# A three-layer fp32 kernel on one core: a new order of weights, exchange and compressed keys, one weight chunk loaded earlier, and modulation sums spread between contraction steps

## What is computed

```python
# layer 1: gated linear attention, 4 heads, chunks of 64 tokens
p = rms_norm(x, pre_norm[0]) @ gla_w_in
q, k, v, glr, z = split(p)
gk = log_sigmoid(glr @ w_gk_up + b_gk) / 16
o = rms_norm(gla_chunked(q, k, v, gk), head_norm) * silu(z)
x = x + rms_norm(o @ gla_w_out, post_norm[0])
# layer 2: sparse attention, 16 heads in 4 groups
p = rms_norm(x, pre_norm[1]) @ nsa_w_in
q, kc, vc, ks, vs, kw, vw, gl, z = split(p)
q, kc, ks, kw = rope(q), rope(kc), rope(ks), rope(kw)
kcmp = silu(blocks(kc, pe_k) @ ck_w1) @ ck_w2      # compressed keys
vcmp = silu(blocks(vc, pe_v) @ cv_w1) @ cv_w2      # compressed values
out = attention over (kcmp, vcmp), (ks, vs) and (kw, vw)
o = sum over the three of sigmoid(gl + b_gate) * out, * silu(z)
x = x + rms_norm(o @ nsa_w_out, post_norm[1])
# layer 3: its input is modulated by a vector c
mod = silu(c) @ w_ada + b_ada          # 1024 -> 3072: shift, scale, gate
h = rms_norm(x, norm_gain) * (1 + scale) + shift
... stick-breaking attention, causal pooling, branches, merge ...
return rms_norm(x + gate * out, final_gain)
```

## Time and profile before

| what | value |
|---|---|
| median of 3 runs | 1273.76 us (1271.89 to 1274.53) |
| profiled execution: time, span of the core | 1273.72 us, 1272.0 us |
| mean granted TensorE clock, share of full speed | 0.99 |
| PE busy | 1229.7 us (97%) |
| PEld busy | 1018.7 us (80%) |
| DVE busy | 641.5 us (50%) |
| ACT busy | 581.6 us (46%) |
| POOL busy | 349.6 us (27%) |
| DMA traffic | 111.68 MB, mean 88 GB/s |

### The profile page before, as it was taken

How to read it: one execution, slowest core, us unless ns; L and a number is a source line. 1 busy time by engine, 2 the same in 40 slices (tenths; PEclk the granted TensorE clock), 3 DMA queues, 4 the chain that set the end, 5 groups by cost and what they waited for, 6 DMA issues and landing times.

```text
span 1272.0 us, 19160 instructions
## 1 busy us (share of the span) xinstructions
PE 1229.7 (97%) x7630; PEld 1018.7 (80%) x7630; DVE 641.5 (50%) x1206; ACT 581.6 (46%) x1127; POOL 349.6 (27%) x172
## 2 busy tenths in 40 slices
PE   7999999898989999899999999999999999999998
PEld 6799868897977755566899888888888788888897
DVE  4487645476466567898735133333333581102434
ACT  4434333524422267788744544444444312434333
POOL 2344420310023211100022422223222553434441
PEclk9999999999989999999999999999999999999999
DMA  7325404454377402100022321222222223332221
GB/s 227 120 67 187 144 1 141 158 157 146 107 135 133 100 20 48 34 2 2 1 67 67 106 83 45 66 67 66 67 68 66 66 99 99 99 116 100 85 82 66
DMA packets 131200, 111.68 MB, mean 88 GB/s; under 512 B 38802, under 2 KB 128016, under 8 KB 131120
## 3 DMA queue, kind: packets, MB, share of 16 engines
q1 hardware_dynamic: 129600, 106.84, 28.7%
q10 hardware_dynamic: 1520, 3.72, 1.3%
HBM read 104.78 MB, written 2.10 MB: 84 GB/s over the span
## 4 chain that ended last, share of the span: by engine, by line
PE 72%; issue 13%; DVE 7%; POOL 4%; ACT 3%; DMA 0%; ACTq 0%; SPq 0%; POOLq 0%; DVEq 0%
PE banks L1260 34%; PE banks L1251 8%; PE banks L1283 5%; POOL w_lo L605 4%; PE banks L1805 3%; PE banks L1657 3%; PE banks L1674 3%; PE banks L1689 3%; PE banks L1712 2%; PE banks L1350 2%; PE banks L1768 2%; DVE w_lo L1908 2%; PE banks L1819 1%; PE banks L1849 1%; PE banks L1227 1%
## 5 line engine op out<-in xcount | busy, mean ns | idle before, releaser
L605 POOL TENSOR_TENSOR w_lo<-raw,w_hi 128x1024 fp32r<-128x1024 f32 x138 | 338.8, 2476 | 831.7 <-ACT w_hi L680 819.7
L1260 PE MATMUL banks<-act_hi,w_hi 128*128 128x512 f32 x704 | 279.0, 396 | 5.2 <-DVE w_lo L1908 5.1
L1260 PE MATMUL banks<-act_hi,w_lo 128*128 128x512 f32 x704 | 276.7, 393 | 0.0
L1260 PE MATMUL banks<-act_lo,w_hi 128*128 128x512 f32 x704 | 276.5, 393 | 0.0
L680 ACT ACTIVATE w_hi<-raw 128x1024 fp32r<-128x1024 f32 (+1 forms) x164 | 162.8, 1042 | 137.0 <-PE banks L1260 87.8
L1260 PEld LDWEIGHTS banks<-act_hi,w_hi 128*128 128x128 f32 x704 | 133.7, 190 | 34.5 <-issue 6.6
L1260 PEld LDWEIGHTS banks<-act_lo,w_hi 128*128 128x128 f32 x704 | 133.6, 190 | 28.5
L1260 PEld LDWEIGHTS banks<-act_hi,w_lo 128*128 128x128 f32 x704 | 133.8, 190 | 27.3
L1251 PE MATMUL banks<-w_hi,act_hi 128*128 128x256 f32 x384 | 109.1, 284 | 0.0
L1251 PE MATMUL banks<-w_hi,act_lo 128*128 128x256 f32 x384 | 108.7, 283 | 0.0
L1251 PE MATMUL banks<-w_lo,act_hi 128*128 128x256 f32 x384 | 108.7, 283 | 0.0
(11 more groups left out here) (379 smaller groups left out, 2371.2 us busy)
## 6 DMA issues: line engine op xcount, KB each, us to landing
raw<-w_in SPq DMA_DIRECT2D x32, 1024.0 KB, 5.7
raw<-gla_w_in SPq DMA_DIRECT2D x11, 1024.0 KB, 5.3
raw<-nsa_w_in SPq DMA_DIRECT2D x33, 256.0 KB, 4.5
raw<-nsa_w_in SPq DMA_DIRECT2D x6, 1024.0 KB, 5.2
raw<-gla_w_out SPq DMA_DIRECT2D x4, 1024.0 KB, 10.9
ada_first<-w_ada SPq DMA_DIRECT2D x4, 1024.0 KB, 8.5
raw<-nsa_w_out SPq DMA_DIRECT2D x16, 256.0 KB, 4.4
raw<-w_branch_a SPq DMA_DIRECT2D x4, 1024.0 KB, 5.1
```

The lines of the kernel that those rows point to most:

```text
L605: pool.tensor_tensor(w_lo[:, u, k], raw[:, u, k], w_hi[:, u, k].bitcast(F32), ALU.subtract).then_inc(lo_done, 1)
L1260: mm = pe.matmul(b[:], w[:, u, k, m * P:(m + 1) * P], x[:, k, :], start=(k == 0 and n == 0), stop=(k == KT - 1 and n == 2))
```

## The change

Five places are edited, all before the attention loop of layer 2.

1. SP loads the third chunk of the output weights of layer 1 (15) directly behind the second, and the fourth (16) ahead of modulation pieces 6 and 7. Before, both stood behind pieces 6 and 7.
2. `modulation` is called piece by piece through a new argument `beside` of `product`, ahead of single contraction steps in the m = 1 half: pieces 0 to 5 in chunk 11, pieces 6 to 9 in chunk 19. Pieces 0 to 5 go to bank 1 in place of bank 4.
3. On ACT the split of chunk 19 stands ahead of `swap_halves(0)`, that of chunk 20 ahead of `swap_halves(2)`, and `swap_halves(4)` moves from behind the split of chunk 22 to behind that of chunk 24. On DVE `turn_parts(C_KW)` moves behind the low parts of chunks 22 and 23.
4. The compressed keys are computed between the two halves of chunk 24, not between chunks 23 and 24. On DVE the low part of chunk 25 moves ahead of the copy of the compressed keys.
5. The first q chunk (28) gets a buffer of its own, `raw_first_q`, in a part of `silu_z2`, and is loaded (four DMAs with runs of 256 bytes) between chunks 23 and 24. The sums of pieces 10 and 11 move from there to `side`.

```diff
@@ SP
                 if c0 == C_GOUT:
                     load(c0, c0 % 2, m, at)
                     load(c0 + 1, (c0 + 1) % 2, m, at + CW)
+                    load(c0 + 2, c0 % 2, m, at + 2 * CW)
                     sp.wait_ge(o_read, 2 * GH)
                     load_row(rows1[:, 0], "post0")
                     load_row(rows1[:, 1], "pre1")
+                    load(c0 + 3, (c0 + 1) % 2, m, at + 3 * CW)
                     sp.wait_ge(h_ready, 2 * KT)
                     load_ada(2)
-                    load(c0 + 2, c0 % 2, m, at + 2 * CW)
-                    load(c0 + 3, (c0 + 1) % 2, m, at + 3 * CW)
                     load_ada(1)
...
                     load(c0, c0 % 2, m, at)
                     if c0 == C_KC:
                         load_ada(1)
+                    elif c0 == C_VS:
+                        sp.wait_ge(ada_summed, ADA_EARLY)
+                        load_heads(w2, N_Q, 0, raw_first_q[:], first_q_landed)
@@ ACT
             def split_high(c, half, u, first=False):
-                if isinstance(c, int) and C_NQ <= c < C_NOUT + 4:
-                    more[u] += 48
-                act.wait_ge(raw_landed[u], 16 * half + 16 + more[u])
+                if isinstance(c, int) and c == C_NQ:
+                    more[u] -= 16
+                    act.wait_ge(first_q_landed, 64)
+                else:
+                    if isinstance(c, int) and C_NQ < c < C_NOUT + 4:
+                        more[u] += 48
+                    act.wait_ge(raw_landed[u], 16 * half + 16 + more[u])
...
+            untaken(C_KS)
             swap_halves(0)
-            untaken(C_KS)
+            split_high(C_VC + 1, (C_VC + 1) // 2, (C_VC + 1) % 2)
             swap_halves(2)
-            split_high(C_VC + 1, (C_VC + 1) // 2, (C_VC + 1) % 2)
             kv_high(0)
...
             untaken(C_CK)
-            swap_halves(4)
             unused_banks(C_CK + 1)
             untaken(C_CK + 1)
 
             hidden_raw(0)
             split_high(C_VW, C_VW // 2, C_VW % 2)
+            swap_halves(4)
             kv_high(1)
@@ PE
                             if m == 0:
                                 weights_ready(c, k)
+                            elif beside is not None:
+                                beside(k)
...
+            def first_sums(k):
+
+                if k == 1:
+                    pe.wait_ge(bank_free[1], (C_Z + 1) // 2 + 1)
+                if 1 <= k <= ADA_GLA:
+                    modulation(k - 1, 1)
+            product(C_Z + 2, (C_Z + 2) // 2, (C_Z + 2) % 2, between=chunk_scores, beside=first_sums)
 
             pe.wait_ge(att_ready, GH)
-            modulation(0, ADA_GLA)
...
-            modulation(ADA_GLA, ADA_EARLY - ADA_GLA)
-
+            def next_sums(k):
+
+                if k < ADA_EARLY - ADA_GLA:
+                    modulation(ADA_GLA + k, 1)
...
-            product(C_VC, C_VC // 2, C_VC % 2)
+            product(C_VC, C_VC // 2, C_VC % 2, beside=next_sums)
...
-            product(C_VW, C_VW // 2, C_VW % 2, by_tokens=True)
+            product(C_VW, C_VW // 2, C_VW % 2, by_tokens=True, between=compressed_keys)
@@ DVE
             turn_sum(2, lambda m: ksT[:, m])
-            turn_parts(C_KW, 4, NDH ** -0.5)
             low(C_CK + 1)
             low(C_VS)
+            turn_parts(C_KW, 4, NDH ** -0.5)
+            low(C_VW)
             turn_sum(4, lambda m: kwT[:, m])
-            low(C_VW)
             kv_low(1)
+            low(C_CV)
             dve.wait_ge(cmp_full, 1)
...
             last.then_inc(cmp_ready, 1)
-            low(C_CV)
             low(C_CV + 1)
```

More of the change, by code:

```diff
@@ L195, in build_program, with raw_of @@
         mod_rows = over("mod_rows", [P, 2, D], silu_z2)
+        def raw_of(c, u):
+            return raw_first_q[:] if isinstance(c, int) and c == C_NQ else raw[:, u]
         def kv_even(part):
@@ L222, in build_program @@
         ada_sum_first = over("ada_sum_first", [P, ADA_EARLY - ADA_GLA, CW], ksT)
-        ada_sum = over("ada_sum", [P, N_ADA - ADA_EARLY, CW], silu_z2, at=silu_z2.manual_sbuf_range[0] + 4 * KT * CW)
+        ada_sum = over("ada_sum", [P, N_ADA - ADA_EARLY, CW], side)
+        raw_first_q = over("raw_first_q", [P, KT, CW], silu_z2, at=silu_z2.manual_sbuf_range[0] + 4 * KT * CW)
         def ada_at(i):
@@ L292, in build_program @@
         turn_ready, turned = sem("turn_ready"), sem("turned")
+        first_q_landed = sem("first_q_landed")
         swap_landed = [sem(f"swap_landed{i}") for i in range(2)]
@@ L487, in _, with load_heads @@
                             load(2 * i + (c0 + u), (c0 + u) % 2, m, 2 * CW * i + (at + u * CW))
+            def load_heads(m, first_col, j, to, landed):
+                for h in range(2):
+                    for g in range(2):
+                        sp.dma_start(to[:, :, h * P + g * NDH:h * P + (g + 1) * NDH],
+                                     cols(m, first_col + j // 2 * 512 + g * CW + (j % 2 * 2 + h) * NDH, NDH)).then_inc(landed, 16)
             for group in groups2:
@@ L679, in split_high @@
                     k = slice(KT // 2 * part, KT // 2 * (part + 1))
-                    act.activation(w_hi[:, u, k, 0:n], raw[:, u, k, 0:n], ACT.Copy).then_inc(hi_done, 1)
+                    act.activation(w_hi[:, u, k, 0:n], raw_of(c, u)[:, k, 0:n], ACT.Copy).then_inc(hi_done, 1)
             def stream(c0, n, take, last=False):
@@ L1232, in product @@
             def product(c, half, u, by_tokens=False, first=False, between=None,
-                        source=(act_hi, act_lo), late=0, middle=None, shared=False):
+                        source=(act_hi, act_lo), late=0, middle=None, shared=False, beside=None):
                 x_hi, x_lo = source
@@ L1475, in modulation @@
                     for m in range(2):
-                        mm = pe.matmul(bank[6 if ADA_GLA <= i < ADA_EARLY else 4][:, 2 * i + m:2 * i + m + 1],
+                        mm = pe.matmul(bank[1 if i < ADA_GLA else 6 if i < ADA_EARLY else 4][:, 2 * i + m:2 * i + m + 1],
                                        ada_at(i)[1][:, m * P:(m + 1) * P], ones[:, 0:1], start=True, stop=True)
@@ L1481, in _ @@
             product(C_Z + 1, (C_Z + 1) // 2, (C_Z + 1) % 2, between=k_d_by_tokens)
-            product(C_Z + 2, (C_Z + 2) // 2, (C_Z + 2) % 2, between=chunk_scores)
+            def first_sums(k):
[4 more added lines that the diff above has]
+            product(C_Z + 2, (C_Z + 2) // 2, (C_Z + 2) % 2, between=chunk_scores, beside=first_sums)
             pe.wait_ge(att_ready, GH)
-            modulation(0, ADA_GLA)
             def first_updates():
@@ L1573, in _, with compressed_keys @@
             product(C_VS, C_VS // 2, C_VS % 2, by_tokens=True, between=lambda: turn_hidden(0))
-            pe.wait_ge(hid_ready, 1)
-            for m in range(2):
-                for half in range(2):
-                    mm = pe.matmul(bank[6][half * NDH:(half + 1) * NDH, 0:NG * NCP], w2k[:, m, :], hid[:, m, :],
-                                   start=(m == 0), stop=(m == 1))
-            mm.then_inc(cmp_full, 1)
-            product(C_VW, C_VW // 2, C_VW % 2, by_tokens=True)
+            def compressed_keys():
+                pe.wait_ge(hid_ready, 1)
+                for m in range(2):
+                    for half in range(2):
+                        mm = pe.matmul(bank[6][half * NDH:(half + 1) * NDH, 0:NG * NCP], w2k[:, m, :], hid[:, m, :],
+                                       start=(m == 0), stop=(m == 1))
+                mm.then_inc(cmp_full, 1)
+            product(C_VW, C_VW // 2, C_VW % 2, by_tokens=True, between=compressed_keys)
             compress(C_CV, 0, 1)
@@ L2014, in _ @@
                                     bank[4 + h][:].rearrange("p (t i) -> p t i", i=P)).then_inc(att_ready, 1)
-            take_mod(0, ADA_GLA, bank[4])
+            take_mod(0, ADA_GLA, bank[1])
             def states_of(h):
@@ L2065, in next_low @@
                 dve.wait_ge(hi_done, 2 * c + part + 1)
-                first_low(c % 2, part)
+                first_low(c % 2, part, c)
             def pre_scaled(t):
```

14 lines of the change are left out of this document (4 added, 10 removed).

## The result

The changed kernel takes 1260.35 us as a median of 4 runs (1257.82 to 1260.75), where four runs of the kernel before gave a median of 1273.62. The ratio is 0.9899, with a 95% interval of 0.9883 to 0.9915: 13 us faster. The forecast was 1261.5, within 1256 to 1267.5.

The account below looks back on a forecast made before the run. PE, busy 97% of the span, was taken as the bound, so only its waits and slow stretches could shorten. Gains 1.0 + 1.0 + 11.8 = 13.8, less one fall of 1.6, net 12.2: 1273.7 to 1261.5 us, range 1256 to 1267.5.

Parts of the forecast that it names:

- one fall of the clock: Two new thin stretches, at chunk 16's first tile and at 357.5 to 361.6; one fall counted, costing 1.6 us.
- A: Sums of pieces 0 to 5 ahead of chunk 12: spreading them avoids a clock fall, 1.6 gained, 0.5 lost, net -1.0.
- the changeovers: Five more changes from narrow to wide matmuls in the spread sums, 0.1 each, 0.5 us lost.
- B's hole: Before the change PE stood still 3.44 and 0.60 us before and in chunk 15; the clock stayed at 1.00.
- B: Chunk 15 loaded early, but POOL slows piece 7's sums; PE waits 3.4 ahead of chunk 16's first tile; net -1.0 us.
- the last sums: Pieces 10 and 11 behind chunk 28: a new PE wait of 0.9 us, and a possible place for a clock fall.
- C: Chunk 19: PE's wait of 1.86 us goes, start at 279.97 where 283.68 was.
- D: Chunk 22: wait of 3.36 us shrinks to a hole of 1.5, with a new one of 1.0 at chunk 23.
- E: Chunk 28: wait of 3.23 us goes; value matmuls start at 358.9 instead of 370.72, -11.8 with C and D.
- rival 3: Slower than before: four q loads ahead of chunk 24 make it land late; over 1276.3 us, chance 0.03.
- Rival 1: No collision of DVE and POOL in B and no fall behind it: -3.4 and -1.6 more, 1256.5 us, chance 0.2.

Follow-up runs that it names:

- A alone: Kernel before with one edit: sums of pieces 0 to 5 spread over steps of chunk 11, in bank 1; 1270.28 us, ratio 0.9970.
- chunk16_behind: Changed kernel with the load of chunk 16 moved behind those of pieces 6 and 7; 1256.40 us, ratio 0.9863.
- first_q_alone: Kernel before with one edit: first q chunk in its own buffer, loaded between chunks 23 and 24; 1270.79 us, ratio 0.9988.
- keys_ahead_of_24: Changed kernel with the compressed keys back between chunks 23 and 24; 1266.16 us, ratio 0.9941.
- pool_waits: Changed kernel with chunk 16's load behind pieces 6 and 7, and POOL's low part of chunk 16 waiting until piece 7 is summed; 1257.04 us.
- weigh_first: Changed kernel with DVE's sum of piece 7 moved behind the two weightings of chunk 14's results; 1256.42 us, ratio 0.9871.
- sums_c_batched: Changed kernel with the sums of pieces 6 to 9 back in one batch ahead of chunk 19; 1256.20 us, ratio 0.9876.
- combined: weigh_first with value matmuls and gate turns between chunk 28's halves, and sums of pieces 6 to 9 batched ahead of chunk 19; 1252.84 us.

## Why the prediction was right

The time lies inside the range, each of the five places came out within 0.5 us of its forecast, and from 150 to 375 us there is one fall of the clock, as counted. The parts in turn.

**A** measured -1.45 where -1.0 was forecast: the first matmul of `updates(0)` starts at 164.15 - 18.50 before and at 163.39 - 19.19 after. The mechanism holds (batch gone, fall gone). The term mis-sized is that of the changeovers: steps with sums are 1.16 apart (150.22 to 151.38) where 0.69 + 0.43 + 0.1 = 1.22 were counted. That A alone brought a fall into B's hole was not foreseen; "which left the clock at 1.00" was no property of that hole.

**B** held term by term. Piece 7's six steps took 7.27 (7.29 taken), the wait was 3.44 (3.4), and it came behind `y_tok`. Counted from the first product the tile started at 233.8 - 18.5 = 215.3 before and at 232.2 - 19.2 = 213.0 after, 2.3 less, of which A has 1.45: B's own -0.9 (-1.0). The fall behind it came as counted (1.75, forecast 1.6), so A and B together were worth only 0.8 at chunk 17 (236.2 and 235.4). The one fall that the forecast counted came here; at the last sums, the other place named, there was none.

The Trainium skill (SBUF — State Buffer, § SBUF: two separate sides) calls the port pair of VectorE and GpSimd an exclusive lock, held for a whole instruction. The traces agree for the six steps, which have two SBUF inputs (7.2 us beside POOL, 3.09 without). In chunk16_behind the single step of 0.35 us ahead of them, with one SBUF tensor and a column of scalars, was held as well: it took 2.12 and ended with POOL's operation (210.98 + 4.76 = 215.74, and 213.76 + 2.12 = 215.88).

**C and D.** Chunk 19 without a wait at 280.0 (279.97), holes of 1.41 and 1.04 (1.5 and 1.0), chunk 28 at 346.67 without one (346.6). That these starts agree to 0.1 us is in part chance: they were forecast on the clock of before, and 0.7 of start-up and the 0.8 won by A and B cancel in them. The distances and the waits agree without that. Chunk 23's hole is its DMA, as said: the chain of after has 5.25 us of `raw<-nsa_w_in` there. The compressed keys had 3.2 us to spare at their place, more than the 1.3 forecast: the silu ended at 326.9.

**E.** 0.44 us of waiting where 0.9 was forecast. The value matmuls started at 359.09 (358.9), and from the first matmul of chunk 17 to that of chunk 29 the distance fell from 118.66 to 107.13, so 11.5 less with A's and B's shifts out of it (11.8 forecast).

**The sum.** At chunk 29 after stands 12.3 us earlier by position (11.6 and the 0.7 of start-up); the forecast was 12.2. The 1.4 that are left come from the attention loop: two falls there before, one after. I let a shift pass through whole and did not count the clock behind it. That term was missing; it was small enough to stay inside the range, by luck and not by the working.

**The rivals.** The q loads of short runs (rival 3) are not harmless: they made a wait of 2.54 in first_q_alone and 2.41 in keys_ahead_of_24, and only the new place of the compressed keys hides it. The price was well below what that rival needed. Rival 1, no collision and no fall behind it, is what pool_waits and weigh_first then made on purpose. Its price was 5.0 us; at chunk 17 they measured 4.4 and 5.2, of which 3.1 and 3.7 were left at layer 3.

**What stays open.** Why a fall comes at one place in one kernel and not in the next. PE's rows around E are alike in the changed kernel, pool_waits (no fall there), sums_c_batched (one), weigh_first and keys_ahead_of_24 (two), which differ there only in when they arrive. The experiments show what falls cost, not where they will be. How they vary between executions shows only in the mean clocks, and not clearly: most runs of the kernel before have 0.987 where the profiled one has 0.990, which would be 3.8 us, and yet they are not slower. And A's place was never undone in the changed kernel, so its share there is read from its rows alone.

## What to carry to other kernels

Read a small change in two parts: what the granted clock of the windows between two matmuls far apart lacks, and the rest of the distance between them. The waits of the changed kernel came out within 0.5 us of a timeline made by hand; between it and its variants the clock's part differed by up to 4.8 us. Ahead of moving a load earlier, ask which engine consumes what it displaces: chunk 15 early was worth nothing until DVE's order or POOL's start was changed too. And edits that look independent may only work together: the q buffer was worth nothing in its trace without the new place of the keys, and undoing either in the changed kernel cost 4.0 and 7.2 us by position (2.2 and 2.4 of it rest, the other part clock).

## What the runs showed of the hardware

- Loads with runs of 256 bytes are slow here. The changed kernel's DMA view from 300 to 320 us has 214 to 220 GB/s while the first q chunk lands, and 344 to 352 while chunk 24 does, behind it.
- A DVE operation on two SBUF inputs, and one on a single SBUF tensor with a column of scalars, are held up while POOL's subtraction runs: six steps of the first kind go from 3.09 to 7.2 us, one of the second from 0.35 to 2.12. A DVE multiplication of a PSUM bank with an SBUF row beside the same POOL operation took its usual 0.69 (weigh_first, at 225.06).
- The clock's share of this kernel went from 11.5 us before to 3.3 after and 0 in combined's profiled execution.
- The start of the first product lies between 16.23 and 19.20 us in the profiled executions, 3.0 apart. The stretch from layer 3's first scores to the end took 549.9 to 550.0 in all of them.
